# Two transformer blocks: where the memory keys' roots and units stand around the latent heads, and two smaller moves

## The reference

```
# first block, layer 1 (the "second mixer"): latent attention, 16 heads
c_q, c_kv, k_r = split(h @ w_in)            # 512, 256, 32 columns
q = rmsnorm(rmsnorm(c_q) @ w_uq)            # per head 64 + 32 columns
k = rmsnorm([rmsnorm(c_kv) @ w_uk, k_r])    # rope on the last 32 columns of q and k
x = x + softmax(causal(q k^T / sqrt(96))) v @ w_out
# then the memory, 4 heads of 256
k, v = split(rmsnorm(mem) @ wkv) per head;  k = rmsnorm(k)
x = x + softmax(rmsnorm(q) k^T / 16) v @ wo
# second block, layer 0, its end: a gate
h = h + (p @ w_proj) * sigmoid(h @ w_gate)
# second block, layer 1 (the "last mixer"): 8 heads of 128, 2 groups of keys and values,
# softmax over the 64 best keys of an index score
```

## Time and profile before

| | |
|---|---|
| median of 3 runs | 2248.14 us (2247.93 to 2248.2) |
| the profiled execution | 2248.48 us, span of the page 2246.7 us |
| PE busy | 2214.4 us, 99% |
| DVE, ACT, POOL busy | 1428.9, 1127.5, 187.1 us |
| weights read | 393.28 MB, 176 GB/s |
| mean granted PE clock | 0.999 |

### The profile page before, as it was taken

How to read it: one execution, slowest core, us unless ns; L and a number is a source line. 1 busy time by engine, 2 the same in 40 slices (tenths; PEclk the granted TensorE clock), 3 DMA queues, 4 the chain that set the end, 5 groups by cost and what they waited for, 6 DMA issues and landing times.

```text
span 2246.7 us, 26156 instructions
## 1 busy us (share of the span) xinstructions
PE 2214.4 (99%) x10574; PEld 1827.5 (81%) x10574; DVE 1428.9 (64%) x1921; ACT 1127.5 (50%) x1683; POOL 187.1 (8%) x219
## 2 busy tenths in 40 slices
PE   9999999999999999999999999999999999999999
PEld 7888888888888887878888888778887888888887
DVE  6655665655565567756555876896557555676556
ACT  6445565545454557655444453434444444464453
POOL 0000000000000020000000980440000000110000
PEclk9999999999999999999999999999999999999999
DMA  7556544556565563336556555425555655536553
GB/s 284 188 188 217 158 130 146 178 187 186 181 223 184 182 202 105 107 120 205 187 187 204 184 185 178 161 83 186 186 187 191 196 186 188 186 109 193 185 188 129
DMA packets 111435, 396.05 MB, mean 176 GB/s; under 512 B 13265, under 2 KB 14033, under 8 KB 111186
## 3 DMA queue, kind: packets, MB, share of 16 engines
q1 hardware_dynamic: 111314, 394.38, 54.7%
HBM read 393.28 MB, written 1.05 MB: 176 GB/s over the span
## 4 chain that ended last, share of the span: by engine, by line
PE 87%; DVE 8%; ACT 3%; issue 1%; DMA 0%; POOL 0%; DVEq 0%; ACTq 0%; POOLq 0%
PE bank L585 27%; PE bank L587 27%; PE bank L586 26%; DVE wlo L1807 3%; PE bank L657 2%; PE bank L646 2%; PE bank L713 1%; PE bank L699 1%; ACT whi L1210 1%; DVE ab_B L2407 0%; DVE bank L2400 0%; DVE bank L2403 0%; PE bank L688 0%; DVE ds_work L2534 0%; PE bank L912 0%
## 5 line engine op out<-in xcount | busy, mean ns | idle before, releaser
L1807 DVE TENSOR_TENSOR wlo<-raw,whi 128x1024 fp32r<-128x1024 f32 (+3 forms) x718 | 877.9, 1261 | 215.7 <-ACT whi L1210 214.1
L1210 ACT ACTIVATE whi<-raw 128x1024 fp32r<-128x1024 f32 (+3 forms) x718 | 721.3, 1049 | 178.5 <-DMA raw<-in_w_w 92.9
L585 PE MATMUL bank<-whi,XH 128*128 128x512 f32 (+3 forms) x1840 | 725.3, 394 | 5.0 <-DVE XL L2448 2.6
L587 PE MATMUL bank<-whi,XL 128*128 128x512 f32 (+3 forms) x1840 | 712.7, 387 | 0.0
L586 PE MATMUL bank<-wlo,XH 128*128 128x512 f32 (+3 forms) x1840 | 711.6, 387 | 0.0
L585 PEld LDWEIGHTS bank<-whi,XH 128*128 128x128 f32 x1840 | 346.3, 188 | 76.5 <-issue 4.8
L587 PEld LDWEIGHTS bank<-whi,XL 128*128 128x128 f32 x1840 | 346.1, 188 | 71.2
L586 PEld LDWEIGHTS bank<-wlo,XH 128*128 128x128 f32 x1840 | 346.7, 188 | 65.5
L585 PE MATMUL bank<-whi,HH 128*128 128x512 f32 x704 | 276.2, 392 | 0.0
L587 PE MATMUL bank<-whi,HL 128*128 128x512 f32 x704 | 274.6, 390 | 0.0
L586 PE MATMUL bank<-wlo,HH 128*128 128x512 f32 x704 | 274.5, 390 | 0.0
(11 more groups left out here) (418 smaller groups left out, 2047.9 us busy)
## 6 DMA issues: line engine op xcount, KB each, us to landing
raw<-in_w_w SPq DMA_DIRECT2D x264, 512.0 KB, 3.5
raw<-in_w_gu_post SPq DMA_DIRECT2D x88, 512.0 KB, 3.6
raw<-in_w_gu_pre SPq DMA_DIRECT2D x87, 512.0 KB, 3.6
raw<-in_w_dn_pre SPq DMA_DIRECT2D x44, 512.0 KB, 3.5
raw<-in_w_dn_post SPq DMA_DIRECT2D x44, 512.0 KB, 3.5
raw<-in_w_x_kv SPq DMA_DIRECT2D x32, 512.0 KB, 4.1
raw<-in_w_sbg_in SPq DMA_DIRECT2D x20, 512.0 KB, 4.4
raw<-in_w_x_q SPq DMA_DIRECT2D x16, 512.0 KB, 4.7
```

Of the source, the lines that this page charges most:

```text
L585: pe.e.matmul(o, xh, hi[:, k, :], start=kt == 0, stop=False)
L587: m = pe.e.matmul(o, xl, hi[:, k, :], start=False, stop=kt == kts - 1)
L1210: act.e.activation(whi[v % SLOTS][:, first:n], raw[v % SLOTS][:, first:n], ACT.Copy).then_inc(*hi_ok.did(v))
L1807: dve.e.tensor_tensor(wlo[v % SLOTS][:, first:n], raw[v % SLOTS][:, first:n], whi[v % SLOTS][:, first:n].bitcast(F32), ALU.subtract).then_ ...
```

## The change

Four things are changed; the computation stays the same.

- In the second mixer `fill(2)` behind `mla_ukv` becomes `fill(4)`, and the heads have units at the eight steps of `ML_FILLS` in place of ten. Behind the first chunk of `mla_ukv` ACT and DVE split two more units, and the roots of the queries and of the first keys are taken at one step.
- Chunk 2 of the memory's keys becomes a "raw" chunk: ACT copies values and unscaled keys out of the banks and squares the keys; root and scaling run at step 15 of the heads. Its turning is put off to chunk 3's. ACT loads the exponential's table ahead of the heads' fence.
- In `ple_g0` the splits ahead at the last chunk go two units less far; the other two come behind "one".
- `divided(name, i)` says at which step which group of heads is divided. For the last mixer the first group is divided at step 7 in place of 6.

```
+BEHIND = {"ple_g0": 2}
             if last:
-                yield "split", rest[-1][0], GROUP
+                yield "split", rest[-1][0], GROUP - BEHIND.get(name, 0)
...
                 if last and j == len(rest) - 1:
                     yield "one", 0
+                    yield "split", rest[-1][0], GROUP
...
-            return lambda c, tiles: [(1, ("kvout", l, c)), (2, ("xk", l, c))] if put_off(l, c) else [(1 if c == 3 else None, ("xk", l, c))]
+            return lambda c, tiles: (([] if raw_keys(l, c) else [(1, ("kvout", l, c))] + [(2, ("xk", l, k)) for k in ((2, 3) if c == 3 else (c,))])
+                                     if put_off(l, c) else [(1 if c == 3 else None, ("xk", l, c))])
+        def raw_keys(l, c):
+            return l == 1 and c == 2
+        def divided(name, i):
+            hpb = 512 // ATT[name]["dv"]
+            back = 4 if name == "ds" and i == hpb + 3 else 3
+            skip = name == "ds" and i == hpb + 2
+            return (i - back) // hpb if i >= 3 and (i - back) % hpb == hpb - 1 and not skip else None
         def put_off(l, c):
-            return l == 1 and c in (0, 3)
+            return l == 1 and c in (0, 2, 3)
+        ML_FILLS = (0, 2, 4, 6, 9, 12, 15, 18)
+        ML_KEYS = 15
...
+        def act_raw_keys(l, c):
+            act.wait_ge(pe_ok, ("xk", l, c - 2))
+            for t in range(2):
+                b = banks.of[(f"x_kv{l}", c), t]
+                act.wait_ge(pe_ok, (f"x_kv{l}", c, t))
+                act.e.activation(XV[l][:, t, c * 256:(c + 1) * 256], b[:, 256:512], ACT.Copy).then_inc(*act_ok.did(("xv", l, c, t)))
+                act.e.activation(XQ[l][:, c % 2, t, :], b[:, 0:256], ACT.Copy).then_inc(*act_ok.did(("xkraw", l, c, t)))
+                act.wait_ge(act_ok, squares[t])
+                squares[t] = ("xks", l, c, t)
+                act.e.activation(junk[:, t, 0:256], b[:, 0:256], ACT.Square, bias=0.0, scale=1.0,
+                                 accum_out=st[:, 18 + t:19 + t]).then_inc(*act_ok.did(squares[t]))
...
             for i in act_run("mla_ukv", out_kv):
                 if i == 0:
+                    act_split_to(act_next[0] + 1)
+                if i == 1:
                     act_sqrt(mlrq[:, :, :], ("mlrq",))
...
-            fill(2)
+            fill(4)
...
+            act_warm(ACT.Exp)
             act_fence("mlatt", 0)
             for i in act_attend("ml"):
-                if i % 2 == 0:
+                if i == ML_KEYS:
+                    act_sqrt(st[:, 18:20], ("xk", 1, 2))
+                if i in ML_FILLS:
                     fill(1, True)
...
+        def dve_raw_keys(l, c):
+            dve.wait_ge(act_ok, ("xks", l, c, 0), ("xks", l, c, 1))
+            dve_var(st[:, 18:20], 1.0 / 256, 1e-6, ("xk", l, c))
+            dve.wait_ge(dve_ok, ("rstd", "xk", l, c))
+            dve.wait_ge(row_in[f"xk{l}"], 0)
+            for t in range(2):
+                x = XQ[l][:, c % 2, t, :]
+                dve.e.scalar_tensor_tensor(out=x, in0=x, scalar=st[:, 18 + t:19 + t], in1=row_of[f"xk{l}"][0], op0=ALU.mult,
+                                           op1=ALU.mult).then_inc(*dve_ok.did(("xk", l, c, t)))
...
             for i in dve_run("mla_ukv", out_kv):
-                keys(i)
-            fill(2)
+                if i == 0:
+                    dve_split_to(dve_next[0] + 1)
+                if i == 1:
+                    keys(0)
+                if i in (1, 2):
+                    keys(i)
+            fill(4)
```

More of the change, by code:

```diff
@@ L718, in pe_attend @@
                             ob[t].open_after = [(dve_ok, ("att", ATT_PIECE[name], g, t))]
-                            turns.append((ATT_PIECE[name], g, t))
                         banks.close(ob)
+                if divided(name, i) is not None:
+                    turns = [(ATT_PIECE[name], divided(name, i), t) for t in range(2)]
                 for x in due:
@@ L726, in pe_kv @@
         def pe_kv(l):
-            yield from pe_run(f"x_kv{l}", lhs_of(f"mem{l}"), lambda c, t: [(dve_ok, ("xk", l, c, t)), (act_ok, ("xv", l, c, t))],
+            yield from pe_run(f"x_kv{l}", lhs_of(f"mem{l}"), lambda c, t: [(act_ok, ("xks", l, c, t))] if raw_keys(l, c) else [(dve_ok, ("xk", l, c, t)), (act_ok, ("xv", l, c, t))],
                               kv_later(l), late=2)
@@ L1343, in act_attend @@
                         m.then_inc(*act_ok.did(*([("exp", name, i)] if t == 1 else [])))
-                if i >= 3 and (i - 3) % hpb == hpb - 1:
-                    turns = [(ATT_PIECE[name], (i - 3) // hpb, t) for t in range(2)]
+                if divided(name, i) is not None:
+                    turns = [(ATT_PIECE[name], divided(name, i), t) for t in range(2)]
                 for x in due:
@@ L1360, in act_keys @@
             act_sqrt(st[:, 6:8], ("xk", l, c))
+        def act_raw_keys(l, c):
[9 more added lines that the diff above has]
+                                 accum_out=st[:, 18 + t:19 + t]).then_inc(*act_ok.did(squares[t]))
         def act_kv(l):
             def out(c, tiles):
-                if not put_off(l, c):
+                if raw_keys(l, c):
+                    act_raw_keys(l, c)
+                elif not put_off(l, c):
                     act_keys(l, c)
@@ L2022, in dve_attend @@
                 dve_settle()
-                if i >= 3 and (i - 3) % hpb == hpb - 1:
-                    h, g = i - 3, (i - 3) // hpb
-                    h0 = h - hpb + 1
+                g = divided(name, i)
+                if g is not None:
+                    h0 = g * hpb
+                    h = h0 + hpb - 1
                     for t in range(2):
@@ L2321, in dve_mla @@
             for i in dve_attend("ml"):
-                if i % 2 == 0:
+                if i == ML_KEYS:
+                    dve_raw_keys(1, 2)
+                if i in ML_FILLS:
                     fill(1, True)
```

## The result

The changed kernel takes **2254.14 us** (median of 6 runs, 2253.74 to 2258.73), the kernel before in the same job 2248.03 us (6 runs, 2246.60 to 2249.26): ratio 1.0034, 95% interval 1.0024 to 1.0044. It is slower by 6.1 us by the medians and by 7.6 by the ratio. The forecast was 2245.8, its range 2241.2 to 2248.6; the prediction was wrong in size and in sign.

The account below looks back on a forecast made before the run. TensorE was taken as the bound, busy 2214.4 of 2246.7 us, so only its gaps and slow clock could be won. Terms 1.15 - 1.4 + 0.2 - 1.4 - 0.8 = -2.3 took 2248.14 to 2245.8 us, range 2241.2 to 2248.6.

Parts of the forecast that it names:

- Behind the heads: Turning of chunk 2's keys moves next to chunk 3's, ahead of the update TensorE waits for; 0.2 us lost.
- the wait at step 11: In the heads, TensorE waits for both divisions because no unit stands at step 10; 2.8 us lost.
- the one that ended slower: Rival: units ahead of the heads and turning run at 1.2 GHz after the 2.35 us wait; 2255.4 us, chance 0.03.
- Ahead of the heads: Roots and two more units between mla_ukv and the turning; sum 1.15 us lost, bounds 2.9 saved to 2.4 lost.
- The new wait for the values' copy: Ahead of the heads, two early splits delay the root and the scalar engine's copy of the values; 2.35 us lost.
- The heads: Old gaps and slow clock go, 5.9 us saved, against new waits of 4.75 less 0.2; sum 1.4 saved.
- step 9: In the heads, head 7's exponential comes late behind chunk 2's copies and squares and a split; 0.9 us lost.
- my second rival: The clock falls again behind the waits of 0.9 and 2.8 us in the heads, costing 1.8; 2247.6 us, chance 0.15.
- The first rival: The new waits in the heads don't arise, 3.7 to 4.5 us more saved; 2241.7 us, chance 0.22.
- Gate: Two of four splits go behind the turning, so TensorE's wait at 1741.07 goes; 1.4 us saved, bounds 0.4 and 1.45.
- Last mixer: First division one step later, so both gaps at 2003 to 2005 go; 0.8 us saved, bounds 0 and 1.6.
- the two waits for divisions: In the last mixer, turnings that need the later divisions, now at step 8, wait 0.6 and 0.3 us.

Follow-up runs that it names:

- e1: The changed kernel with the other bank pair for the first chunk of the second mixer's output, as in the kernel before; 2247.07 us, ratio 0.9997.
- e2: The kernel before with only the other bank pair for the first chunk of the second mixer's output; 2254.25 us, ratio 1.0029.
- e5: e1 without the two early splits behind mla_ukv's first chunk, the root of the queries back at the first step; 2249.83 us, ratio 1.0011.
- e6: e3 without the two early splits behind mla_ukv's first chunk, the root of the queries back at the first step; 2247.38 us, ratio 0.9999.
- e9: e8 with one split put ahead of the heads in place of two; 2245.97 us, ratio 0.9995.
- e11: e10 with one split put ahead of the heads in place of two; 2248.32 us, ratio 1.0003.
- e3: e1 with units of the heads at steps 8 and 10 in place of 9 and 12; 2243.98 us, ratio 0.9992.
- e7: The kernel before with only the last mixer's divisions moved one step later; 2247.81 us, ratio 0.9999.
- e4: The kernel before with only the gate's two splits put behind the turning; 2246.34 us, ratio 0.9996.
- e8: e3 with the last two units at steps 12 and 15 in place of 15 and 18; 2243.03 us, ratio 0.9981.
- e10: e8 with the last unit at step 17 in place of 15; 2246.74 us, ratio 0.9994.

## Why the prediction was wrong

**The step that failed** is the third term of the sum, "Behind the heads": 0.2 lost, "between 0 and 0.6". It measured 7.6, or 7.2 less the 0.44 of work gone from the heads that the term counts. I had priced the work that moves there and had said of the two moved units that they cost nothing by themselves. But opening a chunk also takes a turn of the bank pairs. I had followed the turns up to the value sums of heads 8 to 15, where they bear on the wait at step 11, and stopped one opening short of `mla_out`. The rest could be read ahead of time: DVE's key scaling has its place behind splits and a root, 5 us after the heads' end, in the trace of before as well (935.14), harmless only because nobody wanted that bank. None of my rivals had this in it; the one that ended slower put its loss ahead of the heads, and the units there ran at the full clock in the changed kernel (between 854 and 862 a matmul starts every 0.22 to 0.24 us). e1 and e2 show the cause from both sides. The 7.6 are 5.11 idle, 0.16 of overlap and 2.2 of slow matmuls (935.77 to 940.53 for eleven, 4.76 us in place of 2.53). The 0.44 of the moved turning are in it too, and nearly made up by a wait of 0.22 for a split (933.60 in the kernel before) that is not there.

**Ahead of the heads**, 1.15 lost: measured 0.7. The new wait for the values' copy lost 1.9 (predicted 2.35), the fourth unit started at 862.62 (predicted 863.05), the first score at 873.87. The mechanism was right. What I made of it, that the early splits were a debit, was not: by the traces of e5, e6, e9 and e11 the order costs 1.9 to 2.0 us more without both of them and 1.6 without one, and 1.6 again where the clock falls behind the longer wait.

**The heads**, 1.4 saved: measured 0.2 lost in the changed kernel, and 1.4 saved in e1, where no slow stretch came. All old gaps went. Every new wait came where it was named: step 9 at 0.68 idle (0.9 lost predicted; 0.83 measured with the overlap), step 11 at 2.73 idle (2.8), later 0.28 and 0.41 (0.4 and 0.65). The divisions ended at 908.17, 5.37 us after step 10's start (5.35 predicted). The difference is the clock: my second rival, given 0.15, came true in the changed kernel's profiled execution, at a price of 1.7 (1.8 predicted), and did not in e1's with the very same wait. The first rival fell: the wait at step 11 is real, and e3 shows that the unit at step 10 was its cover.

But the 1.4 was right by luck, for the clock counts on the other side as well. I had booked the old slow stretch of the earlier trace rows as a fixed cost of 1.8 us that the change takes away. e2 and e7 leave the heads of the kernel before as they are, and so does e4. Windows of the kernel before, e4, e2 and e7:

```profile
870.00:930.00 60.00, 56.71 (x336) 48.75 (x336) 38.59 (x91) 42.58 (x112) 0.00 (x0) 0.97 0.25 79
870.00:930.00 60.00, 56.69 (x338) 48.76 (x337) 38.60 (x91) 42.57 (x112) 0.00 (x0) 0.97 0.25 79
870.00:930.00 60.00, 56.00 (x341) 48.29 (x340) 38.62 (x91) 42.75 (x113) 0.00 (x0) 1.00 0.24 79
870.00:930.00 60.00, 56.64 (x343) 48.84 (x342) 39.38 (x93) 42.40 (x112) 0.00 (x0) 1.00 0.25 79
```

All four have the same two gaps (0.65 or 0.66, and 0.77), and in e2 and e7 the full clock stays. There the heads take 60.5 us from the first score to the last unit's end, in the kernel before and e4 61.9. Less the 5.9 of work moved away that is 54.6, and e1 takes 54.5: with the full clock on both sides the new order of the heads saves nothing that could be told.

**Gate**, 1.4 saved: 1.5 in the changed kernel, 1.4 alone in e4's trace. **Last mixer**, 0.8 saved: 0.6 in the changed kernel, and 0.6 alone in e7's trace; the two waits for divisions came as 0.31 and 0.15 against predicted 0.6 and 0.3, yet the last value sums end at 2005.94 (2004.10 and 1.84), not at 2005.45. By the runs neither edit alone can be told from nothing.

e1 is the change as I had understood it. By its ratio of 0.9997 it is 0.7 us under the kernel before (0.1 by the medians), where the sum had 2.3 less with a range of 0.3 to 4.4; its interval, 2.7 us less to 1.3 more, holds the forecast and also no change at all. So the rest of the sum is not refuted by the runs, and not confirmed either; its terms stand by the traces, that of the heads only with the clock's help.

**What stays open.** Why the clock fell behind one wait and not behind its twin was not settled. The end of the heads in e8 (0.85 for the last division) was tried in one other form only, e10, which failed. That chunk 3's keys could be taken out of the banks like chunk 2's, which would make the pair harmless without a hand-set turn, wasn't tried. Nor was the kernel before given the units or the early splits alone, so their worth is known only within the new order. Each experiment has one trace, and the slow stretches differ from trace to trace, so what a single trace shows of the clock is one draw.

## What to carry to other kernels

When work that opens a buffer moves past another opening, every later turn of that buffer shifts: follow the turns to the first user that has a late reader ahead of it, past the end of the stage that the change is about. A reader that is late in the trace but has nobody waiting for it is a wait in store. And price an early piece of work not only by what it holds up but by how many units can run before the next long block of the engine that feeds them. A slow stretch that one trace shows is not a fixed cost: look for it in a second trace of the same code before booking it as a gain.

## What the runs showed of the hardware

The clock after a wait is not a function of the wait alone. e9 and e11 have the same edit ahead of the heads and wait 3.08 and 3.04 us at 858 to 862. Windows of e9, then of e11:

```profile
860.00:865.00 5.00, 3.62 (x11) 2.88 (x12) 5.00 (x6) 2.16 (x3) 0.00 (x0) 0.78 0.20 79
```

```profile
860.00:865.00 5.00, 3.11 (x14) 2.57 (x15) 5.00 (x6) 2.67 (x3) 0.00 (x0) 1.00 0.30 105
```

From the first matmul at 852.61 to the first score at 876.96 are 24.4 us in e9, from 853.13 to 875.86 22.7 in e11: 1.6 us for the slow stretch. The changed kernel and e1 are such a pair as well (2.73 us each, 0.69 and 1.00 behind it), and so are the kernel before and e4 against e2 and e7 (0.65 or 0.66, and 0.77 idle within 2 us). e8 fell to the lower level behind waits of 0.41 and 0.85. The Trainium skill, TensorE: Matmul & The Clock Gate, What's actually happening, says that an idle stretch takes the clock down; these rows agree that it comes behind idle time, and show besides that the same idle time may pass without it. The spread of the runs goes with it: of e3's eleven runs the three with a mean granted clock of 1.000 took 2242.4 to 2244.3 us, the one with 0.996 took 2251.3.
